# Experts' rows for the later passes fetched by an indirect transfer and turned, in place of products with a matrix of places

## The reference

```python
def moe_ffn(h, router_w, w1, w3, w2):
    logits = (h @ router_w).astype(jnp.float32)
    top_vals, top_idx = lax.top_k(logits, TOP_K)          # TOP_K = 2
    top_w = jax.nn.softmax(top_vals, axis=-1)
    gate = jnp.sum(jax.nn.one_hot(top_idx, N_EXPERTS, dtype=jnp.float32) * top_w[..., None], axis=-2)
    out = jnp.zeros_like(h)
    for e in range(N_EXPERTS):
        out = out + gate[..., e:e + 1].astype(h.dtype) * swiglu(h, w1[e], w3[e], w2[e])
    return out
```

## Time and profile before

| | us |
|---|---|
| median of three runs | 2413.31 |
| the profiled execution | 2410.8 |
| its span in the profile | 2409.0 |
| PE busy | 2346.6 (97%) |
| DVE busy | 1695.1 (70%) |
| ACT busy | 1410.2 (59%) |
| POOL busy | 442.3 (18%) |
| PE's share of the chain that ended last | 88% |

### The profile page before, as it was taken

The page is one execution under the profiler, slowest core; times in us unless marked ns, Lnnn a source line. Parts: engine busy times, 40 slices in busy tenths (PEclk is TensorE's granted clock), DMA queues, the critical chain, the costliest instruction groups (busy, mean ns, idle before and its releaser), DMA issues.

```text
span 2409.0 us, 32078 instructions
## 1 busy us (share of the span) xinstructions
PE 2346.6 (97%) x11791; PEld 1943.1 (81%) x11791; DVE 1695.1 (70%) x2242; ACT 1410.2 (59%) x1783; POOL 442.3 (18%) x402
## 2 busy tenths in 40 slices
PE   7999999899998999999999999999999989999998
PEld 7987788798767888888888888788878878887887
DVE  5848755575676988989889898885465548446554
ACT  4543444455434787888888888746454445644443
POOL 2265000004630000000000000085600007560000
PEclk9999999999998999999999999999999999999999
DMA  7535655345346999999999999845475534447450
GB/s 218 193 123 189 222 203 181 107 158 175 110 145 233 367 343 340 366 346 369 340 343 366 344 358 349 296 140 176 161 248 173 194 125 138 168 161 253 168 203 35
DMA packets 384548, 549.75 MB, mean 228 GB/s; under 512 B 27410, under 2 KB 283784, under 8 KB 384312
## 3 DMA queue, kind: packets, MB, share of 16 engines
q1 hardware_dynamic: 380080, 535.82, 65.6%
q0 software_dynamic: 4080, 11.96, 1.6%
q10 hardware_dynamic: 288, 0.59, 0.1%
HBM read 547.28 MB, written 1.05 MB: 228 GB/s over the span
## 4 chain that ended last, share of the span: by engine, by line
PE 88%; DVE 6%; DMA 2%; POOL 1%; ACT 1%; issue 0%; SPq 0%; DVEq 0%; ACTq 0%
PE mb L1042 15%; PE mb L1044 15%; PE mb L1043 15%; PE pb L1042 10%; PE pb L1044 10%; PE pb L1043 10%; DMA ring<-in_w_in 2%; PE pb L1169 2%; PE mb L1435 1%; DVE w_lo L2996 1%; PE pb L1513 1%; PE mb L1196 1%; DVE conv L2349 1%; PE mb L1466 1%; POOL w_lo L858 1%; PE mb L1328 1%
## 5 line engine op out<-in xcount | busy, mean ns | idle before, releaser
L2996 DVE TENSOR_TENSOR w_lo<-ring,w_hi 128x1024 fp32r<-128x1024 f32 x464 | 558.2, 1222 | 165.1 <-ACT w_hi L1908 117.7
L858 POOL TENSOR_TENSOR w_lo<-ring,w_hi 128x512 fp32r<-128x512 f32 x304 | 395.9, 1338 | 1114.7 <-DVE probs L2773 806.5
L1908 ACT ACTIVATE w_hi<-ring 128x1024 fp32r<-128x1024 f32 x360 | 371.6, 1055 | 257.7 <-PE pb L1044 116.0
L1042 PE MATMUL mb<-w_hi,hT_hi 128*128 128x512 f32 x1184 | 473.1, 400 | 0.0
L1044 PE MATMUL mb<-w_lo,hT_hi 128*128 128x512 f32 x1184 | 462.4, 391 | 0.0
L1042 PE MATMUL pb<-w_hi,hT_hi 128*128 128x512 f32 (+1 forms) x976 | 371.7, 381 | 6.3 <-DVE low_rows L2996 3.7
L1044 PE MATMUL pb<-w_lo,hT_hi 128*128 128x512 f32 (+1 forms) x976 | 361.8, 371 | 0.0
L1043 PE MATMUL pb<-w_hi,low_rows 128*128 128x512 f32 (+1 forms) x976 | 361.6, 371 | 0.0
L2996 DVE TENSOR_TENSOR w_lo<-down_w,w_hi 128x1024 fp32r<-128x1024 f32 x242 | 293.0, 1223 | 79.2 <-ACT w_hi L1908 74.8
L2079 ACT ACTIVATE w_hi<-ring 128x1024 fp32r<-128x1024 f32 x256 | 268.1, 1057 | 35.4 <-PE mb L1044 21.1
L1043 PE MATMUL mb<-w_hi,xg_lo 128*128 128x512 f32 x704 | 274.6, 390 | 0.0
(11 more groups left out here) (509 smaller groups left out, 3564.7 us busy)
## 6 DMA issues: line engine op xcount, KB each, us to landing
ring<-in_moe_w SPq DMA_DIRECT2D x128, 1024.0 KB, 9.6
ring<-in_w_in SPq DMA_DIRECT2D x50, 2048.0 KB, 8.0
down_w<-in_moe_w SPq DMA_DIRECT2D x88, 1024.0 KB, 12.3
third_gu<-in_moe_w SPq DMA_DIRECT2D x48, 1024.0 KB, 11.1
down_w<-in_w_ffn_down SPq DMA_DIRECT2D x22, 1024.0 KB, 10.1
ring<-in_w_out SPq DMA_DIRECT2D x8, 2048.0 KB, 8.0
ring<-in_ffn_w SPq DMA_DIRECT2D x16, 1024.0 KB, 7.9
ring<-in_w_ffn_gate SPq DMA_DIRECT2D x16, 1024.0 KB, 5.5
```

Source lines behind the costliest of these rows:

```text
L858: ins = nc.gpsimd.tensor_tensor(w_lo[:, m % NPIECE, cols], source[m][0][:, cols], w_hi[:, m % NPIECE, cols].bitcast(F32), ALU.subtract)
L1042: mm(o, a_hi, hi, start=start, stop=False)
L1908: f(w_hi[:, m % NPIECE], src, ACT.Copy).then_inc(w_hi_ready, 1)
L2996: return tt(dst, src, hi.bitcast(F32), ALU.subtract)
```

## The change

Ahead of the loop POOL writes the 256 rows of `xn` to a tensor in memory, `token_rows`, in two transfers of 512 KiB. In step 4 of each pass PE multiplies `sel` by a column of token numbers, DVE copies the result as 128 integers (`slot_token`), and POOL fetches those 128 rows of 4 KiB with an indirect transfer into `slot_tokens`, a part of the gates' memory that is free then. At the end of the pass `turn_rows(half)` turns them by four transposes per half, at the places where `gather(half)` was. The gather ahead of the loop stays as products.

POOL's list has no loop: it issues `MAXPASS` = 11 indirect transfers, each behind the one before. The loop gives it as many signals as there are passes; behind the loop one DVE instruction (`ts(h_out, ...)`) gives eleven more, so that the rest pass. ACT waits for all of them before it writes gates into the memory they use.

The load of gain 9 moves ahead of the second pair of `bank_root` calls of the layer before. Two semaphores are merged with others.

```diff
+        token_rows = nc.dram_tensor("token_rows", (S, D), F32).ap()
+        slot_tokens = g1[:, 1024:1024 + D]
+        token_no, slot_token = g1[:, 348:350], small[:, 134:135].bitcast(I32)
 ...
@@ POOL
-            pool.wait_ge(quad_ready, 1)
+            pool.wait_ge(table_ready, 2)
 ...
             pool.dma_start(cst2, cdram2[:, :]).then_inc(cst2_in, 16)
+            for i in range(T):
+                pool.dma_start(token_rows[i * P:(i + 1) * P, :], xn[:, i]).then_inc(rows_moved, 16)
+            for t in range(MAXPASS):
+                pool.wait_ge(rows_moved, 16 * (T + t))
+                pool.wait_ge(slots_ready, t + 1)
+                pool.indirect_dma_start(slot_tokens, None, token_rows[:, :],
+                                        bass.IndirectOffsetOnAxis(ap=slot_token, axis=0)).then_inc(rows_moved, 16)
             for l in range(2):
                 L, n = 2 + l, 5 + 4 * l
-                if l:
-                    load_gain(n, a["g_pre_mix_2"][l])
 ...
-                for m in (n + 1, n + 3):
-                    for i in range(T):
-                        bank_root(m, i)
+                for i in range(T):
+                    bank_root(n + 1, i)
+                if l == 0:
+                    load_gain(n + 4, a["g_pre_mix_2"][1])
+                for i in range(T):
+                    bank_root(n + 3, i)
@@ PE
+                def turn_rows(half):
+                    for k in range(4 * half, 4 * half + 4):
+                        ins = turn(mb[2 + half][:, (k % 4) * P:(k % 4 + 1) * P], slot_tokens[:, k * P:(k + 1) * P], ident)
+                    ins.then_inc(gather_mm, 1)
 ...
+                            if c == 4:
+                                pe.wait_ge(sel_ready, t + 2)
                             pe.wait_ge(e_h, t * NF + c)
+                            if c == 4:
+                                for i in range(T):
+                                    mm(mb[3][:, 2 * P:2 * P + 1], sel[:, i], token_no[:, i:i + 1], start=i == 0, stop=i == T - 1)
 ...
                             if c == NF:
-                                pe.wait_ge(sel_ready, t + 2)
-                                gather(0)
+                                pe.wait_ge(rows_moved, 16 * t + 16 * (T + 1))
+                                turn_rows(0)
 ...
-                    gather(1)
+                    turn_rows(1)
@@ ACT
+                if (L, b, h) == (2, 1, 0):
+                    act.wait_ge(rows_moved, 16 * (T + MAXPASS))
@@ DVE
+                ts(h_out, rstd, 1.0, None, ALU.mult).then_inc(slots_ready, MAXPASS)
 ...
-                cp(quad[:, 0:2], place).then_inc(quad_ready, 1)
+                cp(token_no[:, 0:1], const("iotap"))
+                ts(token_no[:, 1:2], const("iotap"), float(P), None, ALU.add)
+                cp(quad[:, 0:2], place).then_inc(table_ready, 1)
 ...
+                            if c == 4:
+                                cp(slot_token, mb[3][:, 2 * P:2 * P + 1]).then_inc(slots_ready, 1)
```

More of the change, by code:

```diff
@@ L518, in build @@
         e_hi_ready, e_split, e_used, xg_hi_ready = (sem(s) for s in ("e_hi_ready", "e_split", "e_used", "xg_hi_ready"))
-        router_in, logits_mm, ex_arg, ex_ready = sem("router_in"), sem("logits_mm"), sem("ex_arg"), sem("ex_ready")
-        both_ready, ranks_mm, quad_ready, quad_moved, table_ready = (sem(s) for s in (
-            "both_ready", "ranks_mm", "quad_ready", "quad_moved", "table_ready"))
+        router_in, logits_mm, ex_ready = sem("router_in"), sem("logits_mm"), sem("ex_ready")
+        both_ready, ranks_mm, quad_moved, table_ready = (sem(s) for s in (
+            "both_ready", "ranks_mm", "quad_moved", "table_ready"))
+        slots_ready, rows_moved = sem("slots_ready"), sem("rows_moved")
         sel_ready, gather_mm, xg_ready, selT_ready, scatter_mm, ys_ready = (sem(s) for s in (
@@ L2060, in experts @@
             def experts():
-                act.wait_ge(ex_arg, 1)
+                act.wait_ge(both_ready, 2)
                 f(ex, ex, ACT.Exp).then_inc(ex_ready, 1)
@@ L3101, in route @@
                 tt(both, one1, one2, ALU.add).then_inc(both_ready, 1)
-                tt(ex, m2, m1, ALU.subtract).then_inc(ex_arg, 1)
+                tt(ex, m2, m1, ALU.subtract).then_inc(both_ready, 1)
                 v.wait_ge(ex_ready, 1)
```

## The result

The changed kernel takes 2422.68 us (median of 11 runs, 2415.23 to 2427.65), the kernel before 2411.57 on the same chip (11 runs, 2408.06 to 2414.76). The ratio is 1.0045 with a 95% interval of 1.0036 to 1.0055: slower by 0.45%, about 11 us (8.7 to 13.3). The profiled execution took 2420.73 with a span of 2418.9.

What follows compares the result with a forecast made beforehand. The prediction took PE as the loop's bound with DMA just behind, DMA taking over after the change. Loop +3.8, behind the loop +2.4, last layer -5.4 sum to +0.8 us: 2414.1 on the median, own range 2409 to 2420, wide range 2394 to 2427.

Steps and rivals of the forecast that it cites:

- Behind the loop: After the loop: three spare transfers make POOL 5.5 us late, so PE waits 1.7 and 0.7 more; +2.4 us.
- pass 1: Second pass of the loop, already bound by DMA: lengthened by one fetch, +1.35 us.
- passes 2 to 7: Six later passes: period goes from 98.3 to 98.5 us as DMA becomes the bound, +1.2 us in all.
- The last gather: End of the last pass: turning in place of the gather lies behind the last step 10, counts in full, -2.66 us.
- The loop changes its bound: In the loop: the bound passes from PE to DMA and the period stays where it was; loop +3.8 us.
- DMA's cycle: Weight loads of a pass, step 10 to step 10: 97.1 us now, 98.5 with the fetch, taken as 1.35.
- The write: Pass 0: writing 1 MiB of rows costs 2.56 us at 410 GB/s; with one fetch, +3.9.
- Rival 1: In the loop: the fetch is hidden and PE stays the bound, the loop gives its 18.1 us, 2392.2; chance 0.22.
- rival 2: In the loop: the fetch costs DMA more than its bytes, 8 x 1.3 = 10.4 us, 2424.5; chance 0.26.
- PE's pass: PE's part of a pass: gather out, turnings and narrow products in, 98.30 to 96.04 us, 2.26 less.
- rival 3: Behind the loop: POOL comes late, its moved splits fall on DVE's work, +10 instead of +2.4, 2421.7; chance 0.08.
- The last layer: Start of the last layer: gain 9 loaded earlier removes DVE's wait for it, -5.4 us (-4 to -6.5).

Runs made afterwards that it cites:

- e7: e3 with 14 of the gate and up products left out of each pass, so PE needs 3.2 us less; 2398.72 us, ratio 0.9946 to the kernel before.
- e6: e1 with 14 of the gate and up products left out of each pass, so PE needs 3.2 us less; 2410.44 us, ratio 1.0000 to the kernel before.
- e8: e1 with each indirect transfer made twice into the same place, 512 KiB more per pass; 2421.0 us, ratio 1.0040 to the kernel before.
- e9: e1 without the two writes of xn to memory, the indirect transfers fetching rows of input x instead; 2407.6 us, ratio 0.9994 to the kernel before.
- e4: e1 with the gather products back in place of the turnings, rows still fetched but unused; 2414.11 us, ratio 1.0016 to the kernel before.
- e1: The changed kernel with 8 indirect transfers instead of 11, without the spare transfers' release and ACT's wait; 2409.2 us, ratio 1.0005 to the kernel before.
- e3: e1 with only the first indirect transfer made, the seven later ones left out, all passes turning those rows; 2406.64 us, ratio 0.9989 to the kernel before.
- e10: e3 with every turning of rows made twice, 0.9 us more PE work per pass; 2405.86 us, ratio 0.9985 to the kernel before.
- e2: The kernel before with only the load of gain 9 moved between the two pairs of roots; 2405.04 us, ratio 0.9981 to the kernel before.

## Why the prediction was right, and where it was not

Forecast 2414.1, measured 2422.7: inside the wide range of 2394 to 2427, above the forecast's own range of 2409 to 2420, and "slower", which had a chance of 0.37, where the sum had about zero. What the loop as a whole does was right. The part behind the loop was not: it was 7.1 us too small, which is most of the miss. Two smaller misses of the sum nearly cancel by luck (pass 1 and passes 2 to 7 together 1.6 too high, the last gather 2.2 too low).

- **The loop changes its bound: right, and shown.** DMA's cycle was put at 97.1 without and 98.5 with the fetch; e7 and e6 show 97.21 and 98.51. The fetch was put at 1.35 and costs 1.30 the first time and 1.19 to 1.29 the second (e8). The write was put at 2.56 and costs about 2.3 (e9). Passes 2 to 7 came out at +0.9 for +1.2. Rivals 1 and 2 are both out: the fetch is not hidden, and it costs no more than its bytes.
- **Pass 1, +1.35: +0.1 (98.82 against 98.75).** The fetch's price is there: e4, with the products and the fetch, has 99.93, 1.2 above the kernel before, and e6 has 98.69 where e7 has 97.66. But without the products pass 1 is 1.1 to 1.6 less than e4's (98.82 here, 98.36 in e1). The step that failed is to count the shorter work of PE as worth nothing in a pass that DMA bounds. Why the products cost that much in pass 1 and 0.3 in a later one is open.
- **PE's pass, 96.04: wrong as a bound.** The instruction prices held: PE is busy 96.31 us. But the step "PE's pass becomes 98.30 - 3.56 + 0.90 + 0.4" took all of the products for work on the path. They also covered two handovers from PE over ACT and DVE back to PE. One is the turned h (`fhT_hi`, `fhT_lo`), the other the rows for the next pass (`xg_hi`, `xg_lo`). Uncovered, they cost 0.57 and 1.29 us (e3; e10 shows that the places are empty; e4 shows them full again). Without any DMA bound the pass would have gained 0.13 us, not 2.26. That the total did not suffer is luck: DMA's cycle stands above 98.16 anyway, by 0.3 us. Rival 1's 2392 was out of reach even with a free fetch.
- **The last gather, -2.66: wrong, -0.5.** The same step failed. PE's wait for `fhT_lo` is new there, and that for `ys_lo` ahead of the scatter went from 0.61 to 1.96. The path runs from the last products over ACT and DVE, not over the gather.
- **Behind the loop, +2.4: the mechanism right, the size too small.** This is what made the kernel slower (e1). POOL was predicted 5.5 late and was 9.2. The sum had 4.6 + 4.2 + 0.8 = 9.6 us for the three transfers, and they took 12.45 (6.2, 5.3 and 0.96). The sum began with the end of DVE's products, but the first issue stands 1572.16 - 1562.37 = 9.8 us behind the scatter, where it had 9.0 (1565.2 against 1556.25). From one issue to the next it took 6.24 and 5.25 us, of which 0.94 is the issue, and the plain load it was priced by took 4.24. The indices are not shown to be the reason. The DMA share was 0.91 and 0.89 in these two stretches and 0.52 in that of the load. And the load of gain 9 itself takes 4.1 us to land in the kernel before but 7.4 in the changed kernel, where it is issued at another place, against 5.0 (median) for the three transfers. What failed is the price, taken from one load with little beside it. The rows are that load before, then after, and the three transfers:

```profile
gain<-in_g_pre_mix POOLq DMA_DIRECT2D x1, 512.0 KB, 4.1
...
gain<-in_g_pre_mix POOLq DMA_DIRECT2D x1, 512.0 KB, 7.4
gates<-token_rows,small POOLq DMA_INDIRECT x3, 5.0
```

  The price of that delay was wrong too: 2.4 for 5.5 late, but 9.5 for 9.2. I let each piece's slack absorb the delay; e1 gives back 9.6 by its ratio and 8.1 in this row of its trace. How the moved splits fell on DVE's work is in the timeline of DVE in the changed kernel, and below it in that of e1:

```profile
1584.09 10.84 DVE L2927 TENSOR_TENSOR u_z<-u_ret 128x384 f32<-128x384 f32 x1
1598.10 9.72 DVE L2329 SCALAR_TENSOR_TENSOR small<-small 128x4 f32<-128x4 f32 x1
...
1593.25 10.87 DVE L2689 SCALAR_TENSOR_TENSOR u_ret<-u_ret,small,ygain 128x256 f32<-128x256 f32 x4 [7.55 <-DMA ygain<-in_g_sgu_v]
```

And PE's wait at the first late piece, then its first product on `u_ret` (before at 1587.94, 31.7 us behind the scatter; now 39.1, and 31.4 in e1):

```profile
1587.19 0.77 PE L1054 MATMUL pb<-w_hi,hT_hi 128*128 128x512 f32 x1 [4.95 <-issue]
1601.51 0.40 PE L1661 MATMUL mb<-cst,u_ret 128*64 128x128 f32 x2 [0.44 <-ACT u_ret L1863]
```

This is rival 3, +10 in place of +2.4, to which I gave 0.08. A wait of PE of 4.95 us stands where I had 1.7; it ends when POOL's first result is due (1584.61 + 2.56 = 1587.17). One DVE operation on 128x4 takes 9.72 us and one on 128x384 takes 10.84 while POOL splits (9.90 us for eight); in e1 the same two kinds take 0.16 and 0.95 to 1.31, and the earlier trace rows already showed it. The chance was too small for what those rows said. But stretching alone loses little: e1 has it on four other DVE operations (10.87 us for what takes 3.49 before), and its row is only 1.5 us over that before. How much of the 9.5 the delay makes, and how much the place where the stretching falls, was not tested apart.

- **The last layer, -5.4: right**, in the trace of the changed kernel and alone in e2 (5.4 in its trace, 4.6 by its ratio).
- **The start, +1.9**, belongs to the spread between profiles. By the ratio the whole difference is 10.9 us, by the spans 9.9.

The parts by their ratios: before 1, the move of the gain 0.9981, the whole change 1.0045. Without the spare transfers it would be 1.0005. So fetching and turning costs about 0.24% against e2 (6 us, of which the write and the first fetch in pass 0 are 2.8 in e1's trace against that of the kernel before), the spare transfers 0.40%.

## What to carry to other kernels

Work on the busiest engine may be the cover of a handover. Before counting its removal, follow what the engine produced just before it, through the other engines, to the next use. If that chain is as long as the work, nothing is gained. When a second cycle stands 1.1 us behind the first (97.2 and 98.3), find it and price it first, as it decides what any saving is worth. And a loop written for the largest count leaves its surplus on the queue behind the loop: the three unneeded transfers cost 9.6 us here (e1), the seven later needed ones 1.7 in the passes (e3 against e1; 3.9 by the ratios, within their noise). A small edit that comes with a large one is worth a run of its own: here it is the only gain.

## What the runs showed of the hardware

The period of the passes rises by about what the bytes of an indirect transfer of 128 rows of 4 KiB take: 1.30 and 1.19 us for 512 KiB (about 400 and 440 GB/s), at a mean rate of 352 to 354 GB/s over the passes. Its issue held POOL for 0.94 us, in the first two passes for 1.55 and 1.77 (and in e8 for 1.82 to 1.90 where it is the second of a pair):

```profile
807.76 1.55 POOL L953 DMA_INDIRECT gates<-token_rows,small  x1 [28.92 <-DVE small L3237]
907.44 1.77 POOL L953 DMA_INDIRECT gates<-token_rows,small  x1 [98.13 <-issue]
```

The next one, waiting for it, followed 6.2 and 5.3 us later. The Trainium skill ("DMA: Bandwidth & Descriptors", section "Anatomy of one DMA") gives an estimate of 3.2 us for the same bytes; these rows are well above it, as is the plain load of gain 9, also 512 KiB, with 4.1 and 7.4 us to land. In the loop the latency made no difference: the fetch is wanted some 59 us later, and e8, where two fetches follow each other 7.25 us apart, lengthens the pass by 1.29. Behind the loop POOL waits for each transfer, and there it did.
